# Seven block products in place of eight in three of eight weight units of the feed-forward up projections

## The reference, cut to what matters

```python
D_MODEL = 2048
SEQ = 256
D_FF = ((8 * D_MODEL // 3 + 255) // 256) * 256      # 5632
def swiglu(hn, w_in, w_out):
    u = hn @ w_in                                   # [256, 2048] @ [2048, 11264]
    return (jax.nn.silu(u[..., :D_FF]) * u[..., D_FF:]) @ w_out
    ...
    h = h + swiglu(rmsnorm(h, norm_ffn[layer]), ffn_w_in[layer], ffn_w_out[layer])
```

## Time and profile before

| | us |
|---|---|
| median of 3 runs (2062.41 to 2063.52) | 2062.68 |
| the profiled execution, its own time | 2061.45 |
| its span, first to last instruction | 2059.7 |
| first up stage, from PE's first to its last matmul there | about 321.0 to 809.8 |
| second up stage | about 1326.1 to 1814.9 |

### The profile page before, as it was taken

The page is one execution under the profiler, slowest core; times in us unless marked ns, Lnnn a source line. Parts: engine busy times, 40 slices in busy tenths (PEclk is TensorE's granted clock), DMA queues, the critical chain, the costliest instruction groups (busy, mean ns, idle before and its releaser), DMA issues. The chain is left out here.

```text
span 2059.7 us, 25451 instructions
## 1 busy us (share of the span) xinstructions
PE 2031.7 (99%) x10171; PEld 1733.6 (84%) x10171; DVE 1095.1 (53%) x979; ACT 917.0 (45%) x894; POOL 91.9 (4%) x113
## 2 busy tenths in 40 slices
PE   7999999999999999999999999999999999999999
PEld 7999988888888888888897888888888888888887
DVE  6868545444444444444466875554444444454543
ACT  5478435333343334343365664443333333334342
POOL 1030200000000000000002320000000000000000
PEclk9999999999999999999999999999999999999999
DMA  7565655555556555655545335465555555555552
GB/s 270 170 199 168 208 197 184 192 195 183 184 184 202 183 189 180 203 191 196 172 147 177 128 102 191 157 216 192 184 191 195 183 184 192 187 192 196 191 192 93
DMA packets 190154, 377.94 MB, mean 183 GB/s; under 512 B 6123, under 2 KB 10485, under 8 KB 189717
## 3 DMA queue, kind: packets, MB, share of 16 engines
q1 hardware_dynamic: 189648, 376.02, 54.9%
q0 software_dynamic: 272, 1.13, 0.2%
q10 hardware_dynamic: 180, 0.05, 0.0%
HBM read 375.08 MB, written 2.10 MB: 183 GB/s over the span
## 5 line engine op out<-in xcount | busy, mean ns | idle before, releaser
L800 DVE TENSOR_TENSOR w_lo<-raw,w_hi 128x2048 fp32r<-128x2048 f32 (+2 forms) x359 | 814.1, 2271 | 765.0 <-ACT w_hi L443 764.5
L443 ACT ACTIVATE w_hi<-raw 128x2048 fp32r<-128x2048 f32 (+2 forms) x359 | 677.7, 1891 | 779.9 <-PE bank L1316 738.5
L1316 PE MATMUL bank<-w_hi,act_hi 128*128 128x512 f32 (+2 forms) x2592 | 1005.0, 388 | 2.9 <-DVE act_lo L805 1.2
L1316 PE MATMUL bank<-w_hi,act_lo 128*128 128x512 f32 (+2 forms) x2592 | 999.5, 386 | 0.0
L1316 PE MATMUL bank<-w_lo,act_hi 128*128 128x512 f32 (+2 forms) x2592 | 999.0, 385 | 0.0
L1316 PEld LDWEIGHTS bank<-w_hi,act_hi 128*128 128x128 f32 x2592 | 486.7, 188 | 98.9 <-DVE act_lo L805 1.9
L1316 PEld LDWEIGHTS bank<-w_hi,act_lo 128*128 128x128 f32 x2592 | 486.6, 188 | 96.5
L1316 PEld LDWEIGHTS bank<-w_lo,act_hi 128*128 128x128 f32 x2592 | 486.8, 188 | 94.4
L1453 PE MATMUL bank<-act_hi,w_hi 128*128 128x256 f32 x512 | 145.5, 284 | 1.4 <-DVE cols L928 0.7
L1453 PE MATMUL bank<-act_hi,w_lo 128*128 128x256 f32 x512 | 144.9, 283 | 0.0
L1453 PE MATMUL bank<-act_lo,w_hi 128*128 128x256 f32 x512 | 144.9, 283 | 0.0
(11 more groups left out here) (175 smaller groups left out, 775.9 us busy)
## 6 DMA issues: line engine op xcount, KB each, us to landing
raw<-in_ffn_w_in SPq DMA_DIRECT2D x176, 1024.0 KB, 5.0
raw<-in_ffn_w_out SPq DMA_DIRECT2D x88, 1024.0 KB, 5.0
raw<-in_lru_w_in SPq DMA_DIRECT2D x32, 1024.0 KB, 5.6
raw<-in_lru_w_out SPq DMA_DIRECT2D x16, 1024.0 KB, 5.0
raw<-in_w_o SPq DMA_DIRECT2D x16, 1024.0 KB, 5.1
raw<-in_w_ukv SPq DMA_DIRECT2D x8, 1024.0 KB, 5.4
raw<-in_w_uq SPq DMA_DIRECT2D x8, 768.0 KB, 4.7
raw<-in_w_dkv SPq DMA_DIRECT2D x8, 576.0 KB, 3.8
```

Source lines behind the costliest of these rows:

```text
L443: A.activation(flat_chunk(w_hi, s, size), flat_chunk(raw, s, size), ACT.Copy).then_inc(w_hi_done, 1)
L800: V.tensor_tensor(flat_chunk(w_lo, s, size), flat_chunk(raw, s, size), flat_chunk(w_hi, s, size).bitcast(F32), ALU.subtract).then_inc(w_lo ...
L1316: i = T.matmul(outs[t], x_part, wp, start=first and n == 0, stop=last and n == 2)
```

## The change

**Units.** A chunk of `w_in` now holds two tiles of the contraction by both halves (tile n of a unit is 0 and 1 for the gate half, 2 and 3 for the up half). Unit u of a block uses x tiles 2u and 2u + 1. A plain unit is 2 x 2 x 2 = 8 block products, 24 matmuls, into four result banks (two position halves by two weight halves). In blocks 1 to 10 the units 2, 4 and 6 (`S_UNITS`) are sum units: the 2x2 block algorithm with seven products, 21 matmuls. It needs four sums of x tiles, made once in a layer (`side`, split to `s_hi`, `s_lo`), and four sums of weight tiles for each unit (`sums` on DVE). The four sums t1 to t4 and the four loaded tiles make seven operands, since t2 takes the place of tile 2. Three of the seven products go to the result banks, four to four shared banks, in which they add up over the three sum units.

**Combining.** After unit 6 ACT copies shared bank 0 out (`p1_done`), and DVE forms the shared sums in four instructions (`shared_out`, ends with `u_done`). After unit 7 DVE adds them to the result banks (`result_out`: two adds, two subtractions), ACT applies SiLU, and DVE multiplies. All eight banks are in use. Banks 0 to 3 are result and banks 4 to 7 shared in even blocks, the other way round in odd ones (`banks_of`), so PE waits for `u_done` of the block before at each block's start.

**Buffers.** In the up stage the low part of the loaded tiles is written over `raw` itself (`raw_lo`, the same memory), since `w_lo` now holds the sums' parts. So a load there waits until PE has used the unit in that slot (`in_place=True`, wait on `chunk_used`).

**Down's first group.** It runs its banks in the order 2, 0, 1, 3, and waits for `u_done`, `r_done` and `gT_act`.

```diff
+S_UNITS = (2, 4, 6)
+FIRST_ORDER = (2, 0, 1, 3)
+S_BLOCKS = FB - 1
...
-            def load(m, s, src, dst=None):
+            def load(m, s, src, dst=None, in_place=False):
                 if not (isinstance(m, int) and m == 0):
-                    sp_.wait_ge(w_lo_done, 4 * m + s - 3)
+                    sp_.wait_ge(chunk_used if in_place else w_lo_done, 4 * m + s - 3)
...
+                for u in range(8):
+                    unit(0, u, slice(0, W), u >= 4)
+                with sp_.Fori(1, FB) as i:
+                    for u in range(8):
+                        unit(i, u, bass.ds(i * W, W), True)
...
+            def split_sums(m, s, q):
+                act.wait_ge(raw_in[s], 16 * m + 16)
+                act.wait_ge(chunk_used, 4 * m + s - 3)
+                A.activation(w_hi[s][:, 0:2, :], raw[s][:, 0:2, :], ACT.Copy)
+                A.activation(w_hi[s][:, 3, :], raw[s][:, 3, :], ACT.Copy)
+                act.wait_ge(t_sum, 3 * q + 1)
+                A.activation(sum_hi_tiles(s)[:, 0:2, :], sum_tiles(t_raw, s)[:, 0:2, :], ACT.Copy).then_inc(sum_hi, 1)
+                act.wait_ge(t_sum, 3 * q + 2)
+                A.activation(w_hi[s][:, 2, :], raw[s][:, 2, :], ACT.Copy).then_inc(sum_hi, 1)
+                act.wait_ge(t_sum, 3 * q + 3)
+                A.activation(sum_hi_tiles(s)[:, 2, :], sum_tiles(t_raw, s)[:, 2, :], ACT.Copy).then_inc(w_hi_done, 1)
...
+                def body(i, odd):
+                    result, shared = banks_of(odd)
+                    for u in range(8):
+                        if u == 0:
+                            gT_out(i - 1, i + FB * f, shared[0:2])
+                        if u == 6:
+                            act.wait_ge(chunk_used, 8 * i + (c0 + 7))
+                            A.activation(gtmp[:, 0, :], shared[0][:, :], ACT.Copy).then_inc(p1_done, 1)
+                        if u == 7:
                             for t in range(NT):
+                                act.wait_ge(c_gate, 2 * i + (2 * S_BLOCKS * f - 1 + t))
+                                k = silu(t, gtmp[:, t, :])
                             k.then_inc(silu_done, 1)
+                        following(i, u)
...
+            def sums(m, s, q):
...
+                V.tensor_tensor(t13[:, 0, :], raw[s][:, 0, :], raw[s][:, 2, :], ALU.add)
+                V.tensor_tensor(t13[:, 1, :], raw[s][:, 2, :], raw[s][:, 3, :], ALU.add).then_inc(t_sum, 1)
+                dve.wait_ge(t_sum, 3 * q + 1)
+                V.tensor_tensor(raw[s][:, 2, :], t13[:, 0, :], raw[s][:, 3, :], ALU.add).then_inc(t_sum, 1)
+                dve.wait_ge(t_sum, 3 * q + 2)
+                V.tensor_tensor(t4, raw[s][:, 2, :], raw[s][:, 1, :], ALU.add).then_inc(t_sum, 1)
...
+                        if u == 6:
+                            shared_out(i, shared)
+                            if isinstance(i, int) and i == FB - 1:
+                                stationary(0, act_slot(0), DOWN_G0[d + 1] + 1)
+                            else:
+                                sums(2 * i + (c0 // 4 + 2), 2, unit_no(f, i + 1, 2))
+                            if not (isinstance(i, int) and i == FB - 1):
+                                continue
+                        if u == 7:
+                            result_out(i, result)
+                            if not (isinstance(i, int) and i == FB - 1):
+                                following(i, 6)
+                        following(i, u)
...
+                        if u == 0:
+                            pe.wait_ge(u_done, i + FB * f)
+                        if u == S_UNITS[0]:
+                            pe.wait_ge(side_lo, f + 1)
+                        pe.wait_ge(w_lo_done, 8 * i + (c0 + u + 1))
+                        if u in S_UNITS:
+                            e = sum_unit(u, result, shared, i + FB * f)
...
+                for u in range(8):
+                    pe.wait_ge(act_lo_done, LO0[d] + max(8, 2 * u + 2))
+                    pe.wait_ge(w_lo_done, c0 + u + 1)
+                    plain_unit(u, ps[0:4], u == 0, u == 7).then_inc(chunk_used, 1)
```

More of the change, by code:

```diff
@@ L454, in act_tiles @@
                                  scale=col(0, gain[kind] + k)).then_inc(act_hi_done, 1)
+                    if kind in (0, 2) and b and q == 1:
+                        for n in range(2):
+                            i = A.activation(side_a[:, b - 1, n, :], hT_psum(b, n), ACT.Copy,
+                                             scale=col(0, gain[kind] + 4 * b + n))
+                        i.then_inc(side_copied, 1)
                     if kind == 1 and q % 2:
@@ L531, in body @@
+                        if u == 5 and isinstance(i, int) and i == FB - 1:
                             stationary(d + 1, 0, act_slot(0))
-                body(0, True)
-                with act.Fori(1, FB - 1) as i:
-                    body(i, False)
+                for u in range(8):
+                    if u == 1:
+                        act_tiles(d, 3)
+                    if u == 3:
+                        act.wait_ge(side_done, f + 1)
+                        A.activation(s_hi, side, ACT.Copy).then_inc(side_hi, 1)
+                    if u == 7:
+                        act.wait_ge(chunk_used, c0 + 8)
+                        act.wait_ge(rstd_done, d + 1)
+                        for t in range(NT):
+                            k = silu(t, ps[2 * t][:, :])
+                        k.then_inc(silu_done, 1)
+                    following(0, u)
@@ L853, in group @@
                                 act_tiles(d, b - 1)
-                        split(g + (DOWN_C[d] // 4 + 1), b)
+                        split(g + (DOWN_C[d] // 4 + 1), b, to=raw_lo if last and d in (0, 2) else w_lo)
                 if DOWN_G[d] > 4:
@@ L894, in up, with gated, following @@
-                body(0, True)
-                with dve.Fori(1, FB - 1) as i:
-                    body(i, False)
+                def gated(t, src):
+                    return V.scalar_tensor_tensor(out=gtmp[:, t, :], in0=src, scalar=stat(RS + 2 * (d + 1) + t),
+                                                  in1=gtmp[:, t, :], op0=ALU.mult, op1=ALU.mult)
+                def following(i, u):
+                    i, u = i + u // 4, (u + 4) % 8
+                    m, s = 2 * i + ((c0 + u) // 4), u % 4
+                    if isinstance(i, int) and i == FB:
+                        if u == 1:
+                            dve.wait_ge(chunk_used, c0 + 8 * FB - 1)
+                        split(m, s)
+                    elif is_sum(i, u):
+                        if u != S_UNITS[0]:
+                            sums(m, s, unit_no(f, i, u))
+                        split_sums(m, s, unit_no(f, i, u))
+                    else:
+                        split(m, s, to=raw_lo)
@@ new lines, in result_out @@
+                def result_out(i, result):
+                    dve.wait_ge(chunk_used, 8 * i + (c0 + 8))
+                    for t in range(NT):
+                        V.tensor_tensor(gtmp[:, t, :], gtmp[:, t, :], result[2 * t][:, :], ALU.add).then_inc(c_gate, 1)
+                    for t in range(NT):
+                        k = V.tensor_tensor(mix[:, t, :], result[2 * t + 1][:, :], mix[:, t, :], ALU.subtract)
+                    k.then_inc(r_done, 1)
+                    dve.wait_ge(r_done, i + S_BLOCKS * f)
+                    dve.wait_ge(silu_done, i + (FB * f + 1))
+                    for t in range(NT):
+                        k = gated(t, mix[:, t, :])
+                    k.then_inc(g_done, 1)
@@ L1338, in transpose_h, with down_block @@
                 i.then_inc(hT_mm, 1)
-            def down_block(d, g, slot, b, first=False, last=False, between=None):
-                if b == 0:
+            def down_block(d, g, slot, b, first=False, last=False, between=None, n=None):
+                n = b if n is None else n
+                if n == 0:
                     pe.wait_ge(st_lo, g + (DOWN_G0[d] + 1))
@@ new lines, in product, with x_tile, plain_unit @@
+            def product(bank, x, w, first, last):
+                for n, (x_part, w_part) in enumerate(((x[0], w[0]), (x[0], w[1]), (x[1], w[0]))):
+                    i = T.matmul(bank[:, :], x_part, w_part, start=first and n == 0, stop=last and n == 2)
+                return i
+            def x_tile(k, t):
+                return tuple(buf[:, k, t * P:(t + 1) * P] for buf in (act_hi, act_lo))
+            def plain_unit(u, result, first, last, ks=(0, 1)):
+                s = u % 4
+                for kk in ks:
+                    for t in range(NT):
+                        for half in range(2):
+                            w = tuple(buf[s][:, 2 * half + kk, :] for buf in (w_hi, raw_lo))
+                            i = product(result[2 * t + half], x_tile(2 * u + kk, t), w, first and kk == 0,
+                                        last and kk == 1)
+                return i
```

274 lines of the change are left out of this document (183 added, 91 removed).

## The result

In runs side by side the changed kernel took 2118.1 us (median of 4, 2115.8 to 2118.5) against 2063.1 us (median of 4, 2062.4 to 2063.9): a ratio of 1.0264, 95% interval 1.0246 to 1.0282, or +55.0 us. The sign was forecast; the time was not. 2085.1 us had been predicted with a range up to 2100.

What follows compares the result with a forecast made beforehand. PE was taken as the bound: -40.8 us of matmuls + 38.9 + 13.5 + 6.6 + 4.2 of waits = +22.4 us on the median 2062.68, giving 2085.1 us, with a range from 2066 to 2100.

Steps and rivals of the forecast that it cites:

- What bounds the kernel, and the gain: Up stages: PE is the bound, busy 99%; 180 matmuls fewer at 0.2267 us each save 40.8 us.
- The chain at the end of blocks 1 to 9: Load, two splits, shared_out: 12.36 us against 10.20 of PE work, so PE waits 2.16 us, 18 times, 38.9 us.
- The last rival: Dearer steps: loads from two halves of w_in land in 5.4 us, 8.8 us more, 2093.9; chance 0.08.
- The forecast gaps: PE's added waits: ends of blocks 1 to 9 38.9 us, block 0 13.5, block 10 6.6, up-stage start 4.2.
- The end of block 0, of block 10 and the start of the stage: PE waits for the gated product 6.76 us, for st_lo 3.3, for act_lo tiles 2.1, each twice.
- the rival about it: PE's clock falls to 1.2 GHz behind block 0's wait, its unit doubling: 10.9 us more, 2096.0; chance 0.06.
- the dearer steps: Block-end chains: loads at 5.4 us plus shared_out instructions at 0.75 in place of 0.68, 2099.5; chance 0.08.
- blocks "above 45": Sign in the profile after: an up block lasting above 45 us would prove the dearer steps; 44.5 was forecast.
- the first rival: Block ends: chain under 10.20 us is hidden, by a faster load or shared_out before the split; 2037.6 us, chance 0.12.

Runs made afterwards that it cites:

- e7_all: Changed kernel with shared_out, SiLU, gated products and stationary work moved earlier, block 0's u_done given earlier, first unit cut by rows: 2023.7 us, ratio 0.9813 to the kernel before.
- e3_loads: Changed kernel with the up-weight loads back to four row tiles of one column half, same amount of work: 2105.0 us.
- e5_block0: Changed kernel with, in block 0 only, SiLU ahead of the copies and gated products ahead of the sums for block 1's unit 2: 2106.0 us.
- e9_gap_silu: e7_all with PE made to wait, at the start of blocks 1 to 10, for the SiLU of the block before: 2167.1 us.
- e10_gap_g: e7_all with PE made to wait, at the start of blocks 1 to 10, for DVE's gated product of the block before: 2199.0 us.
- e1_order: Changed kernel with ACT's copy of shared bank 0 and DVE's shared_out moved ahead of the parts of the next block's unit 1: 2049.1 us, ratio 0.9931 to the kernel before.

## Why the prediction was wrong

**What bounds the kernel, and the gain**: right. The 180 matmuls are worth what was said; e7_all has 38.2 of the 40.8 us, with 2.0 us of waits of its own.

**The chain at the end of blocks 1 to 9**: right in mechanism, place and releaser, 0.4 us short in one step. The load was put at 5.0 us from the row of the same tensor, and measured 5.4. The last rival had named both the size and the form of the load, "the rows of a unit are now drawn from two halves", and got a chance of 0.08; e3_loads shows it was the fact. The prediction said that this costs 22 x 0.4 = 8.8 us. The forecast gaps were 38.9 + 13.5 + 6.6 + 4.2 = 63.2 us; with 8.8 they are 72.0, and the trace has 72.4. That these are so close is in part luck. The forecast counts at each end 0.11 us of a dearer first matmul, which the measured gaps leave out, and in the rows of block 3 above two steps are longer than it had them: 5.55 us from the issue of the load to ACT's split (5.4 even with the correction), and 2.86 us from the start of `shared_out` to PE (2.77). So blocks without a fall of the clock last 45.0 to 45.3 us where 44.9 would follow, and in e3_loads, with the load back at 5.0 us, 44.6 to 44.9 where 44.5 would.

**The end of block 0, of block 10 and the start of the stage**: forecast 6.76, 3.3 and 2.1 us, measured 7.4 and 7.6, 3.3, and 1.8. With 5.4 us for a load the first two would be 7.2 and 3.7; these small misses were not followed up. e5_block0 confirms the cause of the first, e7_all that all three are order.

**The clock**: this is the step that failed. The sum has no term for it, and the rival about it, with a chance of 0.06, weighed it only for the longest wait, because the trace of before had one wait of 2.48 us with no fall behind it, and waits of 2.16 us at block ends were taken as safe without a word. One row was no evidence for 18 waits of about that length, and it was a lucky row: in seven of the eleven kernels the lower clock stood behind this same wait. At the ends of blocks 1 to 9 the clock fell behind 8 of the 18, and over all 13 places it costs 23 us. By the Trainium skill (TensorE: Matmul & The Clock Gate, HAM oscillation — how this bites in real kernels) a matmul loop that waits for its loads again and again gets throttled again and again. The runs agree in part: 0.51 was granted behind the wait shown, but at 2.6 us not every turn had a fall (8 of 18), and at 5 us and more every one did (36 of 36 in e9_gap_silu and e10_gap_g). The prediction had cited that page for block 0 alone, where it applied to the loop.

The price of one fall, on the other hand, was put too high. The rival let the whole unit behind the wait take double, 5.44 us more each time. Windows of the changed kernel behind the wait of the first block 0:

```profile
374.83:379.10 4.27, 4.27 (x10) 3.40 (x11) 4.27 (x4) 0.81 (x1) 0.00 (x0) 0.50 0.00 0
379.20:383.50 4.30, 4.30 (x20) 3.55 (x19) 2.29 (x2) 0.00 (x0) 0.00 (x0) 1.00 0.00 0
```

The lower clock holds for 4.3 us of work, in which 10 matmuls run where 20 run next: about 2.1 us are lost. What was missing were the other eleven places.

**The sum.** -40.8 for the matmuls, +72.4 for gaps, +22.9 for the clock: +54.5. The medians are 55.0 us apart and the two profiled executions 57.0, so 0.5 to 2.5 us stay unexplained. The forecast's +22.4 lacked the 23 us of clock and 9 of gaps. The upper bound of the range put the dearer steps together, but did not add the clock to them: these rivals do not exclude each other, and longer waits make the fall more likely. Of the signs named at its end, blocks "above 45" came true.

**What the prediction had and did not use.** It named the order on DVE, the split ahead of `shared_out`, as what decides for the first rival. Moving it is the edit that wins, and it was in the code for the reading. The price of that rival, 2037.6 us, was wrong for this way to it: it takes 2.16 us off the end of block 0 as well, which only a faster load would do. With the order alone block 0 kept its 7.5 us, and e1_order took 2049.1.

## What to carry to other kernels

When an engine is the bound and a change makes it wait once in every turn of a loop, price the wait twice: its length, and the clock behind it. A wait in a loop is not safe because one like it left no mark before. Where a change frees the bounding engine but ties a load to its progress, write down what stands ahead of each release in the other engines' lists. An instruction whose inputs are ready early, but which stands behind a split that waits for a load, takes on that load's whole latency; moving it forward cost nothing here. Rivals that can occur together have to be added up when the upper end of a range is set.

## What the runs showed of the hardware

The length of a wait and the clock behind it, counted over the profiled runs of all eleven kernels, in the up stages, at their ends, and at the attention's transposes (gaps start to start, less 0.227 us):

| gap of PE, us | gaps | with the lower clock behind |
|---|---|---|
| 1.55 to 2.0 | 37 | 2 |
| 2.0 to 2.5 | 26 | 7 |
| 2.5 to 2.85 | 45 | 22 |
| 3.2 to 3.5 | 9 | 9 |
| over 5 | 46 | 46 |

Between 2 and 3 us the same wait at the same place of the program had it in one block and not in the next; what decides was not worked out here. The attention's wait is the cleanest case: its code is the same in all eleven kernels and it lasts 2.6 to 2.7 us in each. The lower clock stood behind it in seven. Windows behind it, first of the kernel before, then of the changed one:

```profile
1122.98:1126.50 3.52, 3.52 (x25) 3.52 (x26) 1.91 (x5) 1.95 (x3) 0.00 (x0) 1.00 0.24 93
```

```profile
1150.80:1154.00 3.20, 3.20 (x15) 3.20 (x16) 0.42 (x2) 0.42 (x1) 0.00 (x0) 0.50 0.21 80
```

A load of 1 MiB of `w_in` lands 0.4 us later when its rows of 2 KB come from two column halves and two row tiles (5.4 us) than when they come from one half and four row tiles (5.0 us), with the same number of packets (190161 in both runs). Why was not tried. The form alone does not decide it for every tensor: `w_ukv` and `lru_w_in` are loaded as four row tiles of one column range in the kernel before, and land after 5.4 and 5.6 us:

```profile
raw<-in_lru_w_in SPq DMA_DIRECT2D x32, 1024.0 KB, 5.6
```
